# RWKV state products in another order, and the weights of the second expert product made two pieces ahead

## What is computed

```
def rwkv7_step(state, inp):
    r_t, w_t, k_t, v_t, kk_t, a_t = inp
    sk = einsum('bhij,bhj->bhi', state, kk_t)
    state = (state * w_t[:, :, None, :] - sk[..., None] * (kk_t * a_t)[:, :, None, :]
             + v_t[..., None] * k_t[:, :, None, :])
    y = einsum('bhij,bhj->bhi', state, r_t)
    return state, y
...
y = group_norm(y) * ln_x_w + ln_x_b + bonus ; y = y * g
x = x + concat([y_mla, y_rwkv]) @ w_o
...
out = einsum('thk,thkd->td', gate * act, expert_v[idx])      # 16384 experts, 16 chosen for each of 8 heads
```

## Time and profile before

| | us |
|---|---|
| median of 3 runs | 1676.98 |
| lowest and highest | 1675.81, 1677.61 |
| the profiled execution | 1674.47 |
| span of its instructions | 1672.7 |
| PE busy (share of the span) | 1553.9 (93%) |
| PE's weight loads | 1365.8 (82%) |
| DVE busy | 1051.7 (63%) |
| ACT busy | 719.6 (43%) |
| POOL busy | 327.4 (20%) |

### The profile page before, as it was taken

How to read it: one execution, slowest core, us unless ns; L and a number is a source line. 1 busy time by engine, 2 the same in 40 slices (tenths; PEclk the granted TensorE clock), 3 DMA queues, 4 the chain that set the end, 5 groups by cost and what they waited for, 6 DMA issues and landing times.

```text
span 1672.7 us, 25104 instructions
## 1 busy us (share of the span) xinstructions
PE 1553.9 (93%) x10346; PEld 1365.8 (82%) x10346; DVE 1051.7 (63%) x1674; ACT 719.6 (43%) x1223; POOL 327.4 (20%) x151
## 2 busy tenths in 40 slices
PE   7987999999988778989999899999999999999998
PEld 6876788998778657979999899999998777777776
DVE  5565655664498785534999477777775555555554
ACT  4563445553345412144444433333334444444443
POOL 0143000000056130367899300000000000000000
PEclk9998999999999878599999999999999999999999
DMA  7622424555524100135655533333335555555553
GB/s 276 201 91 88 152 101 136 180 192 189 185 89 145 64 2 1 39 113 154 204 172 165 164 114 115 119 118 116 112 112 169 176 177 179 182 180 176 180 182 117
DMA packets 64881, 235.27 MB, mean 141 GB/s; under 512 B 7424, under 2 KB 7680, under 8 KB 64512
## 3 DMA queue, kind: packets, MB, share of 16 engines
q1 hardware_dynamic: 63904, 231.60, 42.9%
q10 hardware_dynamic: 864, 2.07, 0.3%
HBM read 232.60 MB, written 1.05 MB: 140 GB/s over the span
## 4 chain that ended last, share of the span: by engine, by line
PE 73%; DVE 15%; ACT 4%; POOL 3%; issue 3%; DMA 1%; ACTq 0%; DVEq 0%; POOLq 0%
PE ps L129 72%; ACT spl L141 3%; POOL spl L144 3%; DVE Ao L144 2%; DVE spl L144 1%; DVE GE L144 1%; PE ps L138 1%; DVE EB L144 1%; DVE pm L144 1%; DVE prep L144 1%; DVE junk L144 1%; DVE pR L144 1%; DMA raw<-in_w_in_a 1%; DVE be L144 1%; DVE pm L153 1%
## 5 line engine op out<-in xcount | busy, mean ns | idle before, releaser
L141 ACT ACTIVATE spl<-raw 128x1024 fp32r<-128x1024 f32 (+1 forms) x435 | 456.4, 1053 | 652.3 <-PE ps L129 637.9
L144 DVE TENSOR_TENSOR spl<-raw,spl 128x1024 fp32r<-128x1024 f32 (+1 forms) x325 | 395.2, 1222 | 398.7 <-ACT spl L141 398.6
L129 PE MATMUL ps<-xhl,spl 128*128 128x256 f32 x4944 | 610.7, 284 | 11.3 <-POOL spl L144 9.6
L129 PEld LDWEIGHTS ps<-xhl,spl 128*128 128x128 f32 x4944 | 596.5, 190 | 14.9 <-POOL spl L144 11.3
L129 PE MATMUL ps<-spl,Wr 128*128 128x512 f32 x1536 | 376.7, 402 | 3.4 <-DVE Wr L144 3.1
L129 PEld LDWEIGHTS ps<-spl,Wr 128*128 128x128 f32 x1536 | 280.3, 189 | 99.6 <-DVE Wr L144 42.2
L144 POOL TENSOR_TENSOR spl<-raw,spl 128x1024 fp32r<-128x1024 f32 (+1 forms) x110 | 283.7, 2596 | 298.8 <-ACT spl L141 298.5
L129 PE MATMUL ps<-Ao,EB 128*128 128x128 bf16 x768 | 100.7, 296 | 17.7 <-DVE Ao L144 17.3
L129 PEld LDWEIGHTS ps<-Ao,EB 128*128 128x128 bf16 x768 | 83.4, 117 | 27.2 <-issue 25.1
L141 ACT ACTIVATE GE<-ps 128x256 f32<-128x256 f32 (+26 forms) x180 | 56.6, 315 | 96.8 <-DVE GE L144 91.6
L129 PE MATMUL ps<-spl,ahl 128*128 128x512 f32 x384 | 90.1, 396 | 0.0
(11 more groups left out here) (332 smaller groups left out, 1285.7 us busy)
## 6 DMA issues: line engine op xcount, KB each, us to landing
raw<-in_eu SPq DMA_DIRECT2D x128, 512.0 KB, 3.6
raw<-in_ev SPq DMA_DIRECT2D x128, 512.0 KB, 3.5
raw<-in_w_up SPq DMA_DIRECT2D x32, 512.0 KB, 3.5
raw<-in_w_down SPq DMA_DIRECT2D x32, 512.0 KB, 3.5
raw<-in_w_in_a SPq DMA_DIRECT2D x16, 512.0 KB, 5.2
raw<-in_w_pq SPq DMA_DIRECT2D x16, 512.0 KB, 3.4
raw<-in_w_rwkv SPq DMA_DIRECT2D x14, 512.0 KB, 3.6
raw<-in_w_in_t SPq DMA_DIRECT2D x8, 512.0 KB, 3.5
```

What stands on the lines that cost most here:

```text
L129: return Done(self, self.e and self.e.matmul(out, l, r, start=st, stop=sp))
L141: return Done(self, self.e and self.e.activation(out, a, f, bias=bias, scale=scale, accum_out=acc))
L144: return Done(self, self.e and self.e.tensor_tensor(out, a, b, op))
```

## The change

Two things are changed.

1. In the RWKV stage PE, DVE, ACT and POOL take another order. `TAT` goes ahead of `Ut`. The products with the zero state (`u`, `y` of chunk 0) and the state after chunk 3 are no longer made. The products of a state are split in two: `keys(c)` (8 products of keys and values) is issued a step earlier than `state(c)` (8 products with nU), which adds to it. `yo` is split in `out_values` and `out_u` in the same way. The 18 turns are given other places: between the new pieces stand now mT1, mo and the rest, and DVE's `ya` steps come between `take_u` and `next_state`. `finish_y(0)` is run to its end ahead of `sum_y(1)`. POOL fills 64 rows of `yr` with zeros and copies 64 rows of `Ut` to `nU`.
2. In the second expert product ACT and DVE do `weight(0)` and `weight(1)` first, and in step c `weight(c + 2)` and then `w.past("ev", c)`.

```
# PE, in place of the loop over chunks
+            keys(0); state(0); turns.go(); keys(1); turns.go(); turns.go()
+            from_state(1); out_state(1); turns.go()
+            state(1); out_values(0); keys(2); turns.go(); turns.go()
+            from_state(2); out_state(2); turns.go()
+            state(2); out_u(0); turns.go(); turns.go()
+            from_state(3); out_state(3); out_values(1); turns.go()
+            out_u(1); turns.go(); turns.go()
# (written here with several calls on a line)
...
+            def state(c):
+                for r in range(2):
+                    if c:
+                        pe.wait_ge("nU", (c, r))
+                    else:
+                        pe.wait_ge("Ut", 0)
...
+            def out_u(b_):
+                pe.wait_ge("nU", (2 * b_ + 1, 1))
+                if b_ == 0:
+                    pe.wait_ge("nU0")
...
# DVE
+            dve.wait_ge("Ut")
+            next_state(0)
+            for _ in range(3):
+                turns.go()
+            take_u(1)
+            turns.go()
+            next_state(1)
+            turns.go()
+            turns.go()
+            take_u(2)
+            turns.go()
+            next_state(2)
+            sum_y(0)
+            fy = finish_y(0)
+            turns.go()
+            next(fy)
+            turns.go()
+            next(fy)
+            take_u(3)
+            for _ in range(3):
+                next(fy)
+                turns.go()
+            run(fy)
+            sum_y(1)
+            fy = finish_y(1)
# ACT and DVE, second expert product
             weight(0)
+            weight(1)
             for c in range(128):
-                if c + 1 < 128:
-                    weight(c + 1)
+                if c + 2 < 128:
+                    weight(c + 2)
                 w.past("ev", c)
```

More of the change, by code:

```diff
@@ L1071, in tensor @@
                 turns.go()
-            for b_ in range(2):
-                b = pe.bank("Ut", b_)
+            for j in range(2):
+                b = pe.bank("TAT", j)
                 pe.wait_ge("Y_a")
                 pe.wait_ge("Y_v")
[L1076 to L1084, removed]
                 pe.wait_ge("tok", ("a", 1))
@@ L1095, in tensor @@
                 turns.go()
+            for b_ in range(2):
+                b = pe.bank("Ut", b_)
+                pe.wait_ge("MV")
+                for h in range(8):
+                    p = prob(b_, h % 2, h // 2)
+                    last = pe.mm(b[:, h * 64:h * 64 + 64], Y[:, p, :], MV[:, b_, h * 64:h * 64 + 64], True, True)
+                last.then_inc("Ut_ps", b_)
+                pe.give("Ut", b_, "Ut", b_)
+                turns.go()
             pe.wait_ge("TAT")
             pe.wait_ge("tok")
[L1098 to L1106, removed]
-                    for r in range(2):
[L1108 to L1128, removed]
@@ new lines, in of, with keys @@
+            def of(c):
+                return c // 2, slice(64 * (c % 2), 64 * (c % 2) + 64), slice(64 * c, 64 * c + 64)
+            def keys(c):
+                b_, ps, cs = of(c)
+                b = pe.bank("S", c)
+                for r in range(2):
+                    for i in range(4):
+                        hs = slice((2 * i + r) * 64, (2 * i + r) * 64 + 64)
+                        pe.mm(b[64 * r:64 * r + 64, i * 64:i * 64 + 64], ktok[ps, b_, hs], vtok[ps, b_, hs], i == 0, False)
@@ new lines, in state @@
+            def state(c):
+                b_, ps, cs = of(c)
+                b = pe.ps("S", c)
+                for r in range(2):
+                    if c:
+                        pe.wait_ge("nU", (c, r))
+                    else:
+                        pe.wait_ge("Ut", 0)
+                    for i in range(4):
+                        hs = slice((2 * i + r) * 64, (2 * i + r) * 64 + 64)
+                        last = pe.mm(b[64 * r:64 * r + 64, i * 64:i * 64 + 64], btok[ps, b_, hs], (nU if c else Ut)[ps, b_, hs], False, i == 3)
+                last.then_inc("S_ps", c)
+                pe.give("S", c, "S", c + 1)
@@ new lines, in from_state, with out_state @@
+            def from_state(c):
+                b_, ps, cs = of(c)
+                pe.wait_ge("S", c)
+                for r in range(2):
+                    rs = slice(64 * r, 64 * r + 64)
+                    b = pe.bank("u", (c, r))
+                    for i in range(4):
+                        last = pe.mm(b[ps, i * 64:i * 64 + 64], TAT[rs, i, cs], ST[rs, c, i, :], True, True)
+                    last.then_inc("u_ps", (c, r))
+                    pe.give("u", (c, r), "nU", (c, r))
+            def out_state(c):
+                b_, ps, cs = of(c)
+                for r in range(2):
+                    rs = slice(64 * r, 64 * r + 64)
+                    if c in (1, 2):
+                        pe.bank("y", (b_, r))
+                    for i in range(4):
+                        last = pe.mm(pe.ps("y", (b_, r))[ps, i * 64:i * 64 + 64], ARt[rs, i, 1, cs], ST[rs, c, i, :], True, True)
+                last.then_inc("y_ps", c)
+                if c in (1, 3):
+                    for r in range(2):
+                        pe.give("y", (b_, r), "y_in", (b_, r))
@@ L1129, in tensor, with out_values @@
+            def out_values(b_):
                 b = pe.bank("yo", b_)
                 for h in range(8):
[L1131 to L1134, removed]
+                    pe.mm(b[:, h * 64:h * 64 + 64], GK[:, prob(b_, h % 2, h // 2), 128:256], vtok[:, b_, h * 64:h * 64 + 64], h == 0, False)
@@ L1135, in tensor @@
+            def out_u(b_):
+                pe.wait_ge("nU", (2 * b_ + 1, 1))
+                if b_ == 0:
+                    pe.wait_ge("nU0")
+                for h in range(8):
+                    last = pe.mm(pe.ps("yo", b_)[:, h * 64:h * 64 + 64], GB[:, prob(b_, h % 2, h // 2), 128:256], nU[:, b_, h * 64:h * 64 + 64], False, h == 7)
                 last.then_inc("yo_ps", b_)
-                for r in range(2):
-                    pe.give("y", (b_, r), "y_in", (b_, r))
                 pe.give("yo", b_, "y_sum", b_)
+            keys(0)
@@ new lines, in tensor @@
+            state(0)
+            turns.go()
+            keys(1)
+            turns.go()
+            turns.go()
+            from_state(1)
+            out_state(1)
+            turns.go()
+            state(1)
+            out_values(0)
+            keys(2)
+            turns.go()
+            turns.go()
+            from_state(2)
+            out_state(2)
+            turns.go()
+            state(2)
+            out_u(0)
+            turns.go()
+            turns.go()
+            from_state(3)
@@ L1139, in tensor @@
+            out_state(3)
+            out_values(1)
+            turns.go()
+            out_u(1)
+            turns.go()
+            turns.go()
             turns.end("m")
@@ L2178, in vector @@
                 turns.go()
+            for j in range(2):
+                dve.wait_ge("TAT_ps", j)
+                dve.cp(TAT[:, 2 * j:2 * j + 2, :], dve.ps("TAT", j)[:, :].rearrange("p (a b) -> p a b", a=2)).then_inc("TAT", j)
+                turns.go()
             for b_ in range(2):
@@ L2182, in vector @@
                 turns.go()
[L2183 to L2188, removed]
             def finish_y(tb):
@@ L2224, in finish_y @@
                 dve.tt(yB[:, tb, :], yr[:, tb, :], gtok[:, tb, :], ALU.mult).then_inc("yb", tb)
[L2226 to L2243, removed]
@@ new lines, in take_u, with next_state @@
+            def take_u(c):
+                b_, ps = c // 2, slice(64 * (c % 2), 64 * (c % 2) + 64)
+                for r in range(2):
+                    hv = lambda t: t[ps, b_, :].rearrange("p (i r d) -> p i r d", r=2, d=64)[:, :, r, :]
+                    dve.wait_ge("u_ps", (c, r))
+                    dve.tt(hv(nU), hv(Ut), dve.ps("u", (c, r))[ps, 0:256].rearrange("p (i d) -> p i d", d=64), ALU.subtract).then_inc("nU", (c, r))
+            def next_state(c):
+                dve.wait_ge("S_ps", c)
+                new = dve.ps("S", c)[:, 0:256].rearrange("p (i d) -> p i d", d=64)
+                if c:
+                    dve.after(dve.tt(ST[:, c + 1, :, :], new, ST[:, c, :, :], ALU.add).own())
+                    new = ST[:, c + 1, :, :]
+                dve.tt(ST[:, c + 1, :, :], new, bc(Pc[:, :, 64 * c + 63], 2, 64), ALU.mult).then_inc("S", c + 1)
@@ L2528, in finish_y @@
                     yield
[L2530 to L2540, removed]
+            pool.wait_ge("rope2")
+            pool.wait_ge("c_sq")
+            pool.fill(yr[0:64, 0, :], 0.0).then_inc("yr_z")
+            pool.wait_ge("Ut", 0)
+            pool.cp(nU[0:64, 0, :], Ut[0:64, 0, :]).then_inc("nU0")
+            for _ in range(8):
+                turns.go()
+            fy = finish_y(0)
+            for _ in range(4):
+                next(fy)
+                turns.go()
+            run(fy)
+            fy = finish_y(1)
             turns.end("m")
```

33 lines of the change are left out of this document (24 added, 9 removed).

## The result

| | before | changed |
|---|---|---|
| median (4 runs each), us | 1676.39 | 1646.46 |
| lowest and highest | 1674.84, 1677.61 | 1643.80, 1646.69 |
| ratio (95% interval) | | 0.9816 (0.9803 to 0.9829) |
| span of the profiled execution | 1672.7 | 1644.9 |

The change gains 30.8 us by the ratio (28.7 to 33.0), where 23.5 were forecast. By the ratio the new time is 1645.5 beside that median, just under the range's low end of 1646; the median itself is just above it. The product's mechanism came out as described, and in the RWKV stage the outcome of Rival 1; both terms of the sum were too small, that of the RWKV stage by almost half.

A forecast was written before the change was run, and what follows sets the result against it. PE, busy 93% of the span, was taken as the bound, so only its waits and half clock could give time. 1672.7 - 16 (product) - 7 (RWKV) = 1649.7 us span; against the median of runs 1653.5 was forecast, range 1646 to 1662.5.

The forecast's parts named there:

- Rival 1: RWKV stage: full clock through Ut and the chain, 12 us there plus 16 in the product, 1649 us; chance 0.13.
- both terms of the sum: Savings forecast for the two changed stages: 16 us in the second expert product and 7 us in the RWKV stage.
- transfers: Second expert product: buffers freed 0.5 us later make loads the limit, 1713 us at 160 GB/s; chance 0.03.
- the yardstick: Second expert product: w_down's 0.2342 us per matmul interval taken as PE's own pace, giving 359.5 us.
- the 1.5 us put for the start: Second expert product: its first piece stays slow in both kernels, PE idle before it and starting at half clock; 1.5 us.
- 17 to 18: Second expert product: us saved if the pace is that of this stage's unstalled intervals, 0.233 us; 16 was taken.
- the second bound's low point and the first's high point: RWKV stage: half clock 1.8 us behind, full clock 11.4 us ahead; 7 us gained was taken, bounds -2 and +12.
- full-clock list: RWKV stage: clock back before Ut and held until mo of block 1; second w_o group at 702.5, 11.4 us ahead.
- half-clock list: RWKV stage: clock falls in Ut and stays down; second w_o group at 715.7, 1.8 us behind.
- The ledger: RWKV stage: work and waits removed, 8.8 us, plus 1.5 gained, less idle stretches of 3.1 and 1.5; about 6 us.
- The 3.2 us of the last state: RWKV stage: removing the 32 records of the last state, at half clock, was counted as 3.2 us saved.

The follow-up runs named there:

- `before_tat_first`: The kernel before with TAT put ahead of Ut on PE and DVE, nothing else changed; ratio 0.9989 to the kernel before.
- experiments 5 to 8: Changed kernel with Ut first again, 0.9847; kernel before with TAT first, 0.9989; changed kernel with unread matmuls ahead of yA's transposes, 0.9818, or ahead of MV, 0.9803.
- `after_ut_first`: The changed kernel with Ut put ahead of TAT again on PE and DVE; ratio 0.9847 to the kernel before.
- `last_state`: The changed kernel with the 32 unread records of the state after chunk 3 made again, ahead of out_values(1); ratio 0.9829 to the kernel before.

## Why the prediction fell short

**The product: right, sized 2 us too small.** The period, its cause and the cure were as told, and transfers did not become the limit. The term that was off is the yardstick, 0.2342 us from w_down: unstalled intervals in this stage are 0.2324 us (356.8 / 1535). With the 1.5 us put for the start, which this trace has not and six others bear out (358.2 to 358.4), it is 376.6 - 356.8 - 1.5 = 18.3 where the forecast had 15.6, and 17.9 was measured. The text had the better figure as an alternative ("17 to 18"), and the number was chosen from the lower side.

**The RWKV stage: the mechanism right, the choice between two lists wrong.** The step that failed is "from the second bound's low point and the first's high point I take 7 us gained". The two lists were two outcomes of the clock, and a value between them describes neither. Against the traces, in us after MV's start (each list counted from 639.92):

| | full-clock list | half-clock list | measured |
|---|---|---|---|
| mo of block 1, start | 26.2 | 37.1 | 24.8 |
| T, end of block 1's ya | 35.6 | 48.8 | 33.4 |
| second group of w_o | 62.6 | 75.8 | 61.0 |

The first list is Rival 1, at 1649, and it came out, 1 to 2 us better still: 12.4 us measured against its "12". Added to an 18 of the product and set against 1676.4 it gives 1646.0.

**Why I gave that outcome 0.13** was for the most part one misread row. The clock of 0.50 from 670 to 680 "with PE never idle" was held against it. PE wasn't idle in that window, but it had waited just ahead of it, before chunk 1, as the timeline of before has it:

```profile
667.07 0.93 PE L129 MATMUL ps<-pR,TAT 64*64 64x64 f32 x16 [1.07 <-DVE pR L144]
```

The clock fell at 669.5. That wait stands in the prediction as one that the change removes. Its price was put at 1.07 us; what went with it was also the fall behind it. In the changed kernel PE has no wait between 643.09 and the one that ends at 676.58, and the clock, once back at 652.0, stays until 675.9. `before_tat_first` keeps the 1.07 us wait, until 666.17, and its clock falls at 668.9.

Two experiments show the link directly: the wait before MV filled, no fall at 645; the wait before yA filled, no fall at 675.9 but one at 680.9, in the wait behind it. That the fall at 669.5 comes from the wait before chunk 1 rests on these, and on traces with and without it; a wait put back at that place alone was not tried. Nor does every wait bring a fall: PE's waits of 1.1 us until 635.9 in the trace of before and until 639.05 in the changed kernel's, and of 1.43 us until 714.96 there, had none behind them. What tells them from the 1.07 us before chunk 1 stays open. The rule that I cited from the Trainium skill ("TensorE: Matmul & The Clock Gate", "What's actually happening"), that only idle time takes the clock away, agrees with every fall in the RWKV stage of these six traces (before, changed, and experiments 5 to 8): each lies in a wait or begins at most 2.7 us behind one. I was wrong to say that the trace of before did not agree. The section would not lead one to expect a fall behind as little idle time as the 1.07 us ahead of 669.5; there the traces decide. What none of my lists could give is how long half clock lasts: 3.4 to 37.5 us here, with PE busy most of the time.

**Where the 13 us at w_o came from.** 5 us are there by the end of mo (33.3 to 28.3), of which `after_ut_first` puts 4.2 on TAT's place: 1.1 of waits and about 3 of clock. About 8 more lie between mo's end and the last transpose of yA (14.1 us before, 6.5 after): what stood there, state, out_values and keys, is now ahead of mo at full clock, or behind the transposes in PE's wait. That is read from the two timelines; no run takes these 8 us apart. The ledger ("about 6") counted the work and the waits at full price and the clock at nothing.

**What held closely.** DVE and POOL in the changed kernel, with T = 675.84 + 0.69 = 676.5:

```profile
675.84 0.69 DVE L144 TENSOR_TENSOR yA<-yA,mst 128x512 f32<-128x512 f32 x1 [1.75 <-POOL mst L144]
...
682.07 0.42 DVE L144 TENSOR_TENSOR pR<-ps,pR 128x256 f32<-128x256 f32 x1
682.52 2.52 DVE L144 TENSOR_TENSOR pR<-pR,Pc 128x256 f32<-128x256 f32 x1
...
695.94 0.69 DVE L144 TENSOR_TENSOR junk<-ps,junk 128x512 f32<-128x512 f32 x1
...
677.78 6.97 POOL L144 TENSOR_TENSOR spl<-raw,spl 128x1024 fp32r<-128x1024 f32 x3 [1.98 <-ACT spl L141]
...
700.01 1.64 POOL L144 TENSOR_TENSOR yst<-yst,neghalf 128x8 f32<-128x8 f32 x1 [7.55 <-DVE yst L147]
701.62 5.13 POOL L144 TENSOR_TENSOR spl<-raw,spl 128x1024 fp32r<-128x1024 f32 x2
```

The multiplication by the decay ended at 685.04, T + 8.5 (forecast 8.6), held up by POOL's splits: 2.52 us. Block 1's y was added at T + 19.4 (forecast 19.4), the second w_o group began at T + 27.6 (forecast 27). The idle stretches were 3.16 and 1.62 us (forecast up to 3.1 and 3.6). So the chain behind T is DVE's and POOL's, and the time hung on when T came, which hung on the clock.

**What was counted and not there.** The 3.2 us of the last state: 2.0 us at the first and 0.8 at the second w_o group in the trace of `last_state`.

## What to carry to other kernels

Price a wait of the matrix engine with the fall of the clock that can come behind it (not every wait here had one): look for the last wait ahead of every stretch at half clock, not only inside it, and where a change takes that wait away, count what runs behind it at full clock. When two lists differ by one yes-or-no, forecast one of them and give the other its chance, instead of a number in between. In a loop over three engines, find whose queue closes the loop and reorder that one; the same reordering on its neighbour alone made this kernel 1% slower.

## What the runs showed of the hardware

- **A short wait of PE can cost more than itself.** The 1.82 us before MV brought 6.8 us at half clock (13.7 where Ut came ahead of TAT); five unread matmuls in it took this away, and 2.2 us net of the stage. Waits of 1.1 and 1.43 us elsewhere brought no fall.
- **DVE and POOL hold each other up, both ways.** DVE's multiplication by the decay took 2.52 us beside POOL's splits, a pair of its operations 5.56 instead of 1.42; and POOL's root took 2.55 us instead of 1.64 while DVE split a piece. The first direction was forecast, the second was not. An operation of DVE with one input in PSUM was not held up beside the same splits (0.42 us at 682.07, and 2.52 us for the next one, both inputs in SBUF).
- **Unchanged code moves.** MV begins between 639.9 and 643.1 us in the 13 traces in which PE has the same instructions ahead of it.
- **The product's start has two clocks.** With half clock for 3.4 us at its start the product took 358.2 to 359.8 us, without it 356.8.
